# Weight sums spaced by steps, ScalarE's rounding ahead of its wait, and token sums and statistics moved, in a Strassen feed-forward on one core

## The reference

```
mix, state = token_mixers(x, ...)                  # mLSTM heads and windowed attention
x = layer_norm(ALPHA * x + mix @ w_out, ln1_g, ln1_b)
gate, up = split(x @ w_ffn_in, 2)                  # 1024 -> 2 x 2816
x = layer_norm(ALPHA * x + (silu(gate) * up) @ w_ffn_out, ln2_g, ln2_b)
```

## Time and profile before

| | before |
|---|---|
| median of 3 runs | 2397.83 us (2396.9 to 2399.92) |
| the profiled execution | 2399.83 us |
| its span, first to last instruction | 2397.7 us |
| PE busy | 2318.4 us, 97% |
| PEld busy | 2217.1 us, 92% |
| DVE busy | 1544.8 us, 64% |
| POOL busy | 1263.4 us, 53% |
| ACT busy | 1018.3 us, 42% |
| mean granted clock of PE | 0.989 |

### The profile page before, as it was taken

One profiled execution on the slowest core, in us unless ns is written; L12 is line 12 of the kernel. 1 busy time (PEld: TensorE's weight loads), 2 busy tenths in 40 slices (PEclk: granted clock), 3 DMA queues, 4 the chain that ended last, 5 costly groups with the idle time before them and its releaser, 6 DMA issues.

```text
span 2397.7 us, 33613 instructions
## 1 busy us (share of the span) xinstructions
PE 2318.4 (97%) x12621; PEld 2217.1 (92%) x12621; DVE 1544.8 (64%) x2241; ACT 1018.3 (42%) x1683; POOL 1263.4 (53%) x671
## 2 busy tenths in 40 slices
PE   8999999999999999999999899999998999999987
PEld 7899999999999889999999888999988999999986
DVE  4455564555666663678356777777767877677777
ACT  4335554545555433455333232333453344333444
POOL 4455445445455435555455555665455566665552
PEclk9999999999999999999999999999999999999998
DMA  6444434334356765554544555326574322425662
GB/s 209 145 116 135 143 106 144 105 106 140 110 178 197 233 221 182 199 197 172 216 142 147 176 204 190 118 93 232 207 289 145 106 90 95 135 103 205 224 215 93
DMA packets 169670, 387.33 MB, mean 162 GB/s; under 512 B 16830, under 2 KB 104214, under 8 KB 167830
## 3 DMA queue, kind: packets, MB, share of 16 engines
q1 hardware_dynamic: 169510, 385.19, 48.4%
HBM read 308.42 MB, written 77.73 MB: 161 GB/s over the span
## 4 chain that ended last, share of the span: by engine, by line
PE 80%; DVE 9%; DMA 5%; issue 3%; ACT 2%; SPq 1%; ACTq 0%; DVEq 0%
PE acc L287 9%; PE acc L289 9%; PE acc L288 9%; PE acc L2423 8%; PE acc L2419 7%; PE acc L2420 7%; PE fb L2423 4%; PE fb L2419 4%; PE fb L2420 4%; PE kd L2419 4%; PE kd L2420 4%; PE kd L2423 4%; DMA wsum<-in_w 2%; PE fb L643 1%; PE w L633 1%
## 5 line engine op out<-in xcount | busy, mean ns | idle before, releaser
L262 POOL TENSOR_TENSOR wlo<-raw,whi 128x1024 fp32r<-128x1024 f32 x150 | 370.1, 2470 | 459.7 <-ACT whi L256 459.6
L287 PE MATMUL acc<-xh,whi 128*128 128x416 f32 x1200 | 432.0, 360 | 0.1
L289 PE MATMUL acc<-xh,wlo 128*128 128x416 f32 x1200 | 424.2, 354 | 0.0
L288 PE MATMUL acc<-xl,whi 128*128 128x416 f32 x1200 | 421.1, 351 | 0.0
L2183 POOL TENSOR_TENSOR l_wlo<-l_raw,blocks_hi 128x512 fp32r<-128x512 f32 x176 | 254.1, 1453 | 251.3 <-DVE l_raw L2553 163.3
L256 ACT ACTIVATE whi<-raw 128x1024 fp32r<-128x1024 f32 x150 | 158.6, 1057 | 383.9 <-PE acc L289 266.2
L287 PEld LDWEIGHTS acc<-xh,whi 128*128 128x128 f32 x1200 | 226.8, 189 | 8.9 <-issue 6.9
L288 PEld LDWEIGHTS acc<-xl,whi 128*128 128x128 f32 x1200 | 226.8, 189 | 3.0 <-issue 0.2
L289 PEld LDWEIGHTS acc<-xh,wlo 128*128 128x128 f32 x1200 | 226.2, 189 | 2.8
L2419 PE MATMUL acc<-low_r,blocks_hi 128*128 128x416 f32 x608 | 216.6, 356 | 8.2 <-DVE temps L2574 8.0
L2183 POOL TENSOR_TENSOR sums_r<-sums,blocks_hi 128x512 fp32r<-128x512 f32 x132 | 188.5, 1443 | 45.3 <-ACT blocks_hi L2244 34.1
(11 more groups left out here) (523 smaller groups left out, 5767.1 us busy)
## 6 DMA issues: line engine op xcount, KB each, us to landing
l_raw<-in_wB SPq DMA_DIRECT2D x132, 512.0 KB, 3.8
raw<-in_wA SPq DMA_DIRECT2D x110, 512.0 KB, 3.5
hid<-low SPq DMA_DIRECT2D x110, 208.0 KB, 4.2
raw<-in_wB SPq DMA_DIRECT2D x40, 512.0 KB, 4.4
half_R<-in_w SPq DMA_DIRECT2D x24, 704.0 KB, 4.2
half_R<-w2s SPq DMA_DIRECT2D x22, 704.0 KB, 4.3
low<-hid SPq DMA_DIRECT2D x18, 832.0 KB, 7.4
xraw<-in_xT SPq DMA_DIRECT2D x32, 416.0 KB, 5.2
```

The costliest lines, as they stand in the source:

```text
L262: self.nc.gpsimd.tensor_tensor(self.wlo[:, n % 4], self.raw[:, n % 4], self.whi[:, n % 3].bitcast(F32), ALU.subtract).then_inc(self.lo_don ...
L287: pe.matmul(bank[:, 0:TG], hi[:, a], self.xh[x][:, a], start=(a == 0), stop=False)
L288: pe.matmul(bank[:, 0:TG], hi[:, a], self.xl[x][:, a], start=False, stop=False)
L289: last = pe.matmul(bank[:, 0:TG], lo[:, a], self.xh[x][:, a], start=False, stop=(a == KD - 1))
```

## The change

- `w_batch` maps a step n (0 to 153 of the first product) to a batch: batch b is loaded at step 3 + 12b, its two parts are made on DVE at the steps 7 + 12b and 8 + 12b, and it is stored at step 10 + 12b.
- On ACT, in the second product, the piece is rounded ahead of `round_half`, so ahead of the wait for step i.
- `tokens` of pair 2 start two steps later (T1 in step 18, T2 in step 19, T3 and T4 in step 20, remainders from step 21 to 27), and ACT's rounding of them with them.
- Third norm: PE's mean after step 22 in place of 21, centre at 22, squares' sum at 23, variance after step 25 in place of 24; inverse and scale on DVE move from step 24 to the end of step 25, behind the last norm's sum over six tiles; the gain on ACT from step 25 to 26.

```diff
-    W_BATCHES = 12
-    def w_batch(j):
-        return j - 1 if 1 <= j <= W_BATCHES else None
+    W_BATCHES, W_FIRST, W_APART = 12, 3, 12
+    def w_batch(n):
+        b, rest = divmod(n - W_FIRST, W_APART)
+        return b if rest == 0 and 0 <= b < W_BATCHES else None
...
-                if r == 1 and name == "P6" and j and w_batch(j - 1) is not None:
-                    store_weight_pieces(j - 1)
-                if r == 1 and name == "P7" and w_batch(j) is not None:
-                    load_weight_pieces(j)
+                if r == 1 and w_batch(n - 7) is not None:
+                    store_weight_pieces(w_batch(n - 7))
+                if r == 1 and w_batch(n) is not None:
+                    load_weight_pieces(w_batch(n))
...
             for i in range(n):
                 if i < QUARTER:
                     copy_first(r, i)
+                for p, k in pieces_at(r, i):
+                    round_piece(r, p, k)
                 if i == 1:
                     round_half(r, 3)
...
-                for p, k in pieces_at(r, i):
-                    round_piece(r, p, k)
...
-                    round_tokens(2, i - X_AT_HALF[2] - 3)
+                    round_tokens(2, i - X_AT_HALF[2] - 5)
...
-                    if i == 24:
+                    if i == 25:
                         norm_part(8, "variance", 0, 1)
-                    if i == 25:
+                    if i == 26:
                         norm_part(8, "gain", 0, 1)
...
-                if r == 2 and i == 21:
+                if r == 2 and i == 22:
                     norm.take_mean(pe, 8)
-                if r == 2 and i == 24:
+                if r == 2 and i == 25:
                     norm.take_variance(pe, 8)
...
-            if i == 1:
+            if i == (1, 0)[r - 1]:
                 dve.wait_ge(S["x_in"], 16 * X_IN[r])
                 if r == 2:
                     dve.wait_ge(y_out, 16)
                 nc.vector.tensor_tensor(raw["T1"], b12, raw["B11"], ALU.subtract).then_inc(t_made, 1)
+            if i == 1:
                 dve.wait_ge(t_made, done + 1)
...
-                tokens(2, i - X_AT_HALF[2])
+                tokens(2, i - X_AT_HALF[2] - 2)
...
-                    if name == "P1" and j and w_batch(j - 1) is not None:
-                        sum_weights(j - 1, name)
-                    if name == "P3" and w_batch(j) is not None:
-                        sum_weights(j, name)
+                for part_of in range(2):
+                    if r == 1 and w_batch(n - 4 - part_of) is not None:
+                        sum_weights(w_batch(n - 4 - part_of), part_of)
...
-            if i == 21:
+            if i == 22:
                 norm_part(8, "centre", 0, 2)
                 norm_part(8, "centre", 1, 2)
-            if i == 22:
+            if i == 23:
                 norm_part(8, "sum_sq", 0, 1)
-            if i == 24:
-                norm_part(8, "invert", 0, 1)
-                norm_part(8, "scale", 0, 1)
             if i == 25:
                 dve.wait_ge(S["evac"], evacuated(2, 25))
                 over_some(last_total, x[:, 0:KD - 2]).then_inc(norm.summed, 1)
+                norm_part(8, "invert", 0, 1)
+                norm_part(8, "scale", 0, 1)
```

More of the change, by code:

```diff
@@ L2025, in store_done, with load_weight_pieces, store_weight_pieces @@
             sp.dma_start(io["z"][g, :, 4 * k + j], x_tiles(r, w, j)).then_inc(z_out[w], 16)
-        def load_weight_pieces(j):
-            jj, k = divmod(w_batch(j), len(CUTS))
+        def load_weight_pieces(batch):
+            jj, k = divmod(batch, len(CUTS))
             a, b = CUTS[k]
-            if w_batch(j):
-                sp.wait_ge(w_out, W_OUT + 64 * w_batch(j))
+            if batch:
+                sp.wait_ge(w_out, W_OUT + 64 * batch)
             for i, n in enumerate((2 * (QUARTER + jj), 2 * (QUARTER + jj) + 1, 2 * jj, 2 * jj + 1)):
                 sp.dma_start(wsum[:, i, 0:b - a], io["w2"][n, :, a:b]).then_inc(w_in, 16)
-        def store_weight_pieces(j):
-            jj, k = divmod(w_batch(j), len(CUTS))
+        def store_weight_pieces(batch):
+            jj, k = divmod(batch, len(CUTS))
             a, b = CUTS[k]
-            sp.wait_ge(w_made, W_MADE + 4 * (w_batch(j) + 1))
+            sp.wait_ge(w_made, W_MADE + 4 * (batch + 1))
             for i, s in enumerate((2, 0, 1, 3)):
@@ L2610, in hidden, with sum_weights @@
                     signal(nc.vector.tensor_tensor(t4_tile, b21_tile, t2, ALU.subtract))
-        def sum_weights(j, name):
-            n = w_batch(j)
+        def sum_weights(n, part_of):
             a, b = CUTS[n % len(CUTS)]
             a21, a22, a11, a12 = (wsum[:, i, 0:b - a] for i in range(4))
-            if name == "P1":
+            if part_of == 0:
                 dve.wait_ge(w_in, 64 * (n + 1))
@@ L2621, in sum_weights @@
                 nc.vector.tensor_tensor(a21, a11, a21, ALU.subtract).then_inc(w_made, 1)
-            if name == "P3":
+            else:
                 dve.wait_ge(w_made, W_MADE + 4 * n + 2)
@@ L2784, in vector @@
                     last_sum(r, j + 1)
-                if r == 1:
-                    if name == "P1" and j and w_batch(j - 1) is not None:
-                        sum_weights(j - 1, name)
-                    if name == "P3" and w_batch(j) is not None:
-                        sum_weights(j, name)
+                for part_of in range(2):
+                    if r == 1 and w_batch(n - 4 - part_of) is not None:
+                        sum_weights(w_batch(n - 4 - part_of), part_of)
                 norm_part(6, *pair_part(r, j, name))
```

## The result

| | before | after |
|---|---|---|
| median of the runs | 2398.88 us (2396.9 to 2400.43, 4 runs) | 2372.26 us (2368.71 to 2375.45, 4 runs) |
| the profiled execution, its span | 2399.83, 2397.7 us | 2370.58, 2368.8 us |
| mean granted clock of PE | 0.989 | 0.989 |

The ratio is 0.9888, 95% interval [0.9875, 0.9900]: 26.6 us less, where 43.7 were forecast. The time lies above the range of 2348 to 2364. Direction and main term were right; four smaller terms, one of which the sum did not have at all, were wrong, all to the same side. What follows compares profiled executions stage by stage.

The account below looks back on a forecast made before the run. PE sets the time, losing it in waits, mostly on DVE. Gains 29.7 + 2 x 3.2 - 1.4 + 9.4 - 0.4 = 43.7 us take 2399.83 to 2356.1; the median, 2.0 lower, gives 2354 us, range 2348 to 2364.

Parts of the forecast that it names:

- Weight sums: Pair 1's first product: loads ordered four steps ahead end DVE's waits and PE's stalls; gain 29.7 us, bounds 25 and 30.2.
- Rival 1: Pair 1's first product: additions crowd DVE and push joins past PE's slack, leaving 10 to 15 us of gain; chance 7%.
- rival 5: Weight loads still land after 9.2 us because SP is held by `spill` waits; 2359 to 2364 us; chance 6%.
- Rounding, steps 15 and 16: Second products of both pairs: pieces rounded before the wait remove late weights and a late third piece; 3.2 us each.
- Step 20: Pair 1's second product: stall inside goes, stall before grows as weights land only 1.4 us earlier; net loss 1.4 us.
- Step 24: Pair 1's second product: later tokens' sums free DVE, which waits 2.8 us for each of three POOL operations; gain 9.4 us.
- The token remainders end 3 to 5 us behind step 27: End of pair 1's second product: harmless, as the last is needed 9 us on, in the next stage's fifth step.
- Third norm: Pair 2's second product: PE's 5.2 us stall goes, tail starts 1.1 us earlier, slow clock costs 1.6; net loss 0.4.
- the first two or three of the five: Kernel's end: that many of the last five statistics run at 1.2 GHz after 7 us of idleness, losing 1.6 us.
- rival 3: Kernel's end: all five last statistics run at 1.2 GHz, 2.0 us more than in the sum, 2356 us; chance 15%.
- Rival 2: Pair 1's second product: DMA backlog at step 20 and DVE's queue at 24 keep half of 16.6 us; 2360 to 2363; chance 14%.
- Rival 4: Second products: ACT waits for piece loads before rounding weights, stalling PE at up to eleven places; slower than before; chance 2%.

Follow-up runs that it names:

- the run with the join first: The changed kernel with the token remainder of step 26 made in step 27, behind that step's join: 2367.69 us, ratio 0.9873.

## Why the prediction was right and wrong, point by point

- **Weight sums: right.** 29.7 us forecast, 27.7 measured (355.0 where I said 352 to 354), with the clock at 1.00 and no wait of DVE for a load. Of the 2 us that lack, 1.7 are three steps (48, 120, 132) at 2.86 to 2.90 us in place of 2.29, which wait for ACT's `blocks_hi`; I hadn't priced these. The reason was half right: the prediction gives the four steps of lead the main credit and SP's wait for the store a part, and the spacing did nearly all of it. Rival 1 (DVE crowded) and rival 5 (loads still late) did not occur.
- **Rounding, steps 15 and 16: right**, 3.2 us in each pair, shown by the run that undoes it. In pair 1 they did not last, as the next point says.
- **Step 20: the step that failed is "these weights land only about 1.4 us earlier".** The forecast was a net loss of 1.4 us; steps 19 and 20 together went from 15.89 to 20.23 us, 4.3 lost. The weights landed 16.2 us after their issue, not 12.6, and so no earlier in the stage (130.9 us after its first matmul, before 130.6): all of the 3.2 us that steps 15 and 16 gave came back as waiting. PE lost 5.3 us before step 20 where 3.5 were forecast, and step 20 lost 2.3 us by the clock (8.60 us) where 1.2 were. The prediction has no row for the 1.4 us; they need room in the DMAs ahead of these weights, and there was none. By the windows of the changed kernel (columns of the earlier trace rows), four stretches of 4 us, the first of them while a norm's result is being stored:

```profile
1720.00:1724.00 4.00, 4.00 (x23) 3.94 (x22) 2.01 (x2) 2.87 (x2) 0.10 (x1) 1.00 0.95 275
...
1732.00:1736.00 4.00, 4.00 (x23) 3.93 (x22) 2.50 (x2) 1.25 (x1) 3.15 (x1) 1.00 1.02 418
...
1740.00:1744.00 4.00, 0.00 (x0) 0.00 (x0) 2.27 (x2) 0.54 (x1) 0.00 (x0) 0.88 1.03 418
1744.00:1748.00 4.00, 3.07 (x9) 2.97 (x10) 1.92 (x2) 2.21 (x2) 3.09 (x1) 0.50 1.02 419
```

  The share of busy DMAs is 0.95 at 275 GB/s and 1.02 at 418: at 275 they were nearly as full. None of the eight windows of 4 us from 1716 to 1748 is under 0.95. PE stands still from 1740 to 1744, and its clock is 0.50 in the next 4 us. The wait table puts this stall (5.2 us) down to "DVE low L2665". PE needs ACT's rounding of these weights, and ACT's timeline names what that waited for:

```profile
1743.46 1.38 ACT L2232 ACTIVATE half_H_r<-half_S 128x1408 fp32r<-128x1408 f32 x1 [10.19 <-DMA half_S<-w2s]
```

  The load is also the one whose removal from behind the inputs takes the stall away.
- **Step 24: the step that failed is "waits about 2.8 us for each of three POOL operations".** 9.4 us forecast, 4.8 measured (16.38 to 11.54). There were four such waits. With four in place of three the prediction's 22.9 us for DVE's stretch become 25.7; it took 25.3 (1753.7 to 1779.1), and PE waited 3.5 us for the third piece. The step lost 5.25 us: the other 1.75 are the lower clock behind the wait, for which the term had nothing. In the run with the join first, whose kernel is the same up to there, PE waited 3.5 us too, the clock stayed at 1.00, and step 24 took 9.98 us. The Trainium skill (SBUF — State Buffer, "SBUF: two separate sides") has the rule of the exclusive lock, and the sentence in the prediction that counted four by it gave a loss of 3.5 us. The two timelines agree with the rule. I should have let the stretch after step 20 hold as many waits as POOL has operations there, one a step.
- **Start of pair 2: a step was missing.** "The token remainders end 3 to 5 us behind step 27, the last is asked for only in the next stage's fifth step" looked at who reads the remainders, and not at what is queued behind them: the join of step 27, which frees a bank for PE's second step. Costed at nothing, it took 3.5 us; the run with the join first gives all of it back.
- **Third norm: right in its mechanism, wrong in the size of two terms ("the tail starts 1.1 us earlier", "the first two or three of the five").** The wait for `total` went, DVE's queue did forbid an earlier tail, ACT's squares stood directly behind the gains, and PE stood idle for 7.6 us (7 forecast) before the last statistics. Steps 15 and 16 gave 3.2 us to this stage and yet it is 0.2 longer: 3.4 lost where I forecast 0.4. By the timelines ACT's squares began 183.6 us after the stage's first matmul (2343.74), before 186.8 (2376.02): earlier by steps 15 and 16 alone, and not by the 1.1 us more that I forecast, since PE waited 0.9 us in step 24 for ACT's `half_T_r` and reached step 25 that much later. From the squares to the sum of the root (DVE L2832) it was 11.3 us, before 8.4: 2.8 for the clock, where I had two or three pairs at 1.2 GHz and 1.6 us (rival 3, all five, was nearer here; over the executions with the same idle time it was two, three and four, so which of the two comes nearer is luck). From there to the end it was 13.8 and 13.2 us; for this 0.6 I have no cause. The Trainium skill (TensorE: Matmul & The Clock Gate, "What's actually happening") says that activity has to release the clock; the prediction's reading of it, that none of the five pairs is released, did not come true: the rows show four slow ones, and the fifth at 0.88 us.
- **Sum.** The spans differ by 28.9 us, 14.8 less than the 43.7 forecast. The terms lack 2.0 (weights), 2.9 (step 20), 4.6 (step 24), 3.5 (pair 2's start) and 3.0 (tail), 16.0 in all, and the part ahead of pair 1 happened to be 1.0 shorter; 0.2 is rounding. By the medians 17.1 us lack, the rest being the spread of the executions. Two small slips stand in the prediction's own sums, and neither matters: 22.9 less 22.0 is a loss of 0.9 and not 0.7 us, and 1.1 less 1.6 is -0.5 and not -0.4. Rival 2 (14%) named the two stalls that came, but not the start of pair 2 and only part of the tail, so its 2360 to 2363 was too low as well; and of the 16.6 us that it halves 3.2 belong to steps 15 and 16. Rival 4 (slower) did not occur.

## What to carry to other kernels

When a stall goes, the next limit is where the saved time must arrive. Here a load behind full DMAs did not land earlier because it was asked for 3 us earlier, and the busy share of the DMAs, not GB/s, said that they were full. When a producer and its loads wait for each other in a ring, as the sums, their store and the next load did, widen the ring first (27 us) and the lead after (0.7). For every operation that is moved to a later place, list what is queued behind it on its engine at the place where it lands, above all across the border to the next stage. And where several producers feed one end, move the one that sets it (here DVE's sum, 6.9 us) rather than the one that waits for it (PE's mean, which cost 3.1 us). Two parts of a change may be worth something only together (4.3 us here, where each alone gave 0.1 and 0.7), so undo them one by one and all at once.

## What of the hardware was not expected

- At 275 GB/s the DMAs were nearly as full (0.95) as at 418 GB/s (1.02).
- After 7.6 us of idleness PE ran two, three or four pairs at 1.2 GHz, by the execution (four: 5.7 us from the first pair to the fifth); after 0.4 us, none.
- The join that reads PSUM took 0.57 us at 1763.31 while POOL was working (L2668); the one behind it, with both inputs in SBUF, took 3.02 (L2670).
